# Four seven-product steps per panel, a six-slot ring in the feed-forward stage, and 36 low halves made by an accumulating transfer

## The chip, the cores and the metric

One Trainium2 chip, one core. The metric is device time in microseconds of one execution of the whole program, from inputs in HBM to the output in HBM. The kernel before takes 3272.08 us (median of 3 runs, 3271.72 to 3272.53). The matrix engine is called PE here, VectorE DVE, ScalarE ACT, GpSimd POOL; SP issues the loads.

## What is computed

Three transformer blocks over 256 tokens of width 2048, all in float32: two layers of the first kind, one of the second. Cut to what matters:

```python
def hybrid_layer(x, mem, ...):                 # twice
    u = rms_norm(x, norm_g) @ w_in             # 2048 -> 15944 columns
    ...                                        # four branches a, b, c, m on 512 columns each
    for n, (y, z) in enumerate(...):
        branch = y * silu(z)
        merged += sigmoid(gate_all[:, :, n]) * (branch @ w_branch[n])   # gates: 4 x 2048 columns of u
    return x + merged @ w_out

def hybrid_layer_2(x, ...):                    # once
    ...                                        # two attentions, gates, w_o
    gt, up = split(rms_norm(x, g_ffn) @ w_gate_up)    # 2 x 5632 columns
    return x + (silu(gt) * up) @ w_down
```

Every weight is used once, on 256 tokens. 610 MB come in from HBM.

## The kernel before

**The work is a stream of chunks.** `stream()` (L76) lists blocks of weight columns in the order of use. A plain block is 512 columns wide and is loaded in chunks of two 128-row tiles, 128x1024 elements, 512 KB. PE works in float32r. So that the product has float32's accuracy, each chunk is split: ACT rounds it to float32r into `w_hi` (L1148), and DVE writes the remainder, raw minus `w_hi`, into `w_lo` (L1452). Three matmuls then stand for one exact one: high by high, low by high, high by low (L1127, and `three`, L1044, in panels). A chunk of a plain block is 2 row tiles x 2 token tiles x 3 = 12 matmuls of 512 columns.

**Panels.** 19 blocks are panels, 1024 columns wide: five in each of the two layers (gates of branches c, m, b; `("panel", l, br, n)`) and nine in the feed-forward stage (`("panel", FF, "f", j)`, 512 columns of gate beside 512 of up). A panel has 16 row tiles, taken as eight steps of two. A step is a 2x2 by 2x2 product of tiles: 128 tokens twice, two row tiles, 512 columns twice. In the plain form it takes 8 products, 24 matmuls, as two units `row` of 12. In the seven-product form (Winograd's) it takes 7 products, 21 matmuls, as four units: `low` (6 matmuls), `first` (3), `sums13` (6) and `sums24` (6). Its price lies elsewhere: DVE makes four sums of weight tiles (`sums13` L1434, `sums24` L1439 and L1440), and these are split like other chunks. In elements per partition a plain step has 2048 to split, a seven-product step 3584, beside the 2048 of sums. Steps 1, 3 and 5 have this form before (`SEVEN`, L35). The token side needs sums too, "forms": POOL makes them (`x_forms`, L1852), ACT rounds them (L1392), DVE writes the remainder (`form_lo`, L1755), once for each layer and once for the feed-forward stage, and PE waits for all of them at the first unit of the first panel (L1071).

**The order of a stage.** In the layers a panel is followed by two merge blocks of two chunks each (`branch @ w_branch` for the 1024 columns whose gates the panel made), then the next panel: one "layer period". In the feed-forward stage down block j-2 (four blocks of two chunks: 8 chunks) comes before panel j: one "feed-forward period" is 8 down chunks and a panel. Before the first of these panels stand gate and up of j = 0 and 1 as plain blocks, then the down blocks of j = 0.

**Rings.** Raw chunks and split chunks lie in rings of four slots. From the first panel of a layer to its last merge the rings have six (`wide`, L136; `in_slots`, L185): the two further slots lie over memory that is idle then. A unit is split into the slot that the oldest unit leaves, so ACT and DVE may run 4 (or 6) units ahead of PE and no more. SP issues a load when the split that read its raw slot is done, and waits in order for that (L712 to L714).

**Work behind a unit.** `schedule()` (L223) lists by unit number what else is to be done. PE does it right behind that unit. ACT and DVE do it behind the split for which they had to wait for PE to finish that unit (`BEHIND`, L212), so four or six units later in their own order. This holds for the work at the end of a panel too: `stem` (ACT), `cross` (DVE L1457 to L1460), `gather` (DVE L1469), `silu_product` (L1475, L1479), the merges (L1541, L1543) and the adds of the down blocks (L1513). The forms of the feed-forward stage stand at `end_of("up", 0) + 4 + 6 * i` (L312).

**Counters.** `hi_done` and `lo_done` count the splits, `mm_done` the units that PE has finished. A wait for unit c's low half is `lo_done >= c + 1`.

Of the kernel before, what the change touches and what calls it, by code (L numbers as in the profile page):

```python
# [7 lines left out]
F32 = mybir.dt.float32  # L8
# [6 lines left out]
P = 128  # L15
# [4 lines left out]
H = 4  # L20
# [13 lines left out]
STEPS = KD // 2  # L34
SEVEN = (1, 3, 5)  # L35
N_FF = 5632 // NB
FF, FF_PLAIN = 3, 2
PANEL_EVENTS = (0, 1, FF)
HEADS2 = 8
NOPE, ROPE2 = 128, 64  # L40
# [15 lines left out]
class Block:  # L56


    def __init__(self, name, weights, col, pair, kk, kt, kind, width=NB):
        self.name, self.weights, self.col, self.pair = name, weights, col, pair  # L60
        self.kk, self.kt, self.kind, self.width = kk, kt, kind, width
        self.ck = 1 if width == WIDE else CK if width == NB else kt // 2
        self.first = 0
        self.wide = False
        self.g = self.before = None

    @property
    def chunks(self):
        return sum(4 if s in SEVEN else 2 for s in range(STEPS)) if self.kind == "panel" else self.kt // self.ck

# [5 lines left out]
def stream():  # L76
# [56 lines left out]
    for b in out:  # L133
        b.first = at
        at += b.chunks
        b.wide = (b.kind == "panel" and b.name[1] != FF) or (b.name[0] == "merge" and b.name[1] < DEPTH and ("panel", *b.name[1:3], b.name[3] // 2) in panels)  # L136
        b.before = tuple(uses)
        if b.kind == "panel":
            uses = [n + 1 for n in uses]
            g = 1  # L140
        else:
            g = b.g = 1 - g
            uses[g] += 1
# [7 lines left out]
def in_units():  # L151

    units, loads = [], []
    for b, blk in enumerate(BLOCKS):
        if blk.kind != "panel":
            for s in range(blk.chunks):
                units.append((b, "plain", s, len(loads)))
                loads.append((b, s))
            continue
        for s in range(STEPS):  # L160
            k0 = len(loads)
            loads += [(b, 2 * s), (b, 2 * s + 1)]
            if s in SEVEN:
                units += [(b, "low", s, k0 + 1), (b, "first", s, k0), (b, "sums13", s, None), (b, "sums24", s, None)]
            else:
                units += [(b, "row", 2 * s, k0), (b, "row", 2 * s + 1, k0 + 1)]
    return units, loads
# [11 lines left out]
LAST_PANEL = {l: max(b for b in PANELS if BLOCKS[b].name[1] == l) for l in PANEL_EVENTS}  # L179
FORMS_DONE = {l: len(SEVEN) * (i + 1) for i, l in enumerate(PANEL_EVENTS)}  # L180
FF_PANEL = {b: i for i, b in enumerate(b for b in PANELS if BLOCKS[b].name[1] == FF)}
STEM_ENDS = {SUMS_UNIT[b, SEVEN[-1]]: b for b in PANELS}

# [28 lines left out]
BEHIND = {c: range(max(R_BEHIND[c], 0), R_BEHIND[c + 1]) for c in range(N_CHUNKS)}  # L212
EXT_FIRST = {l: [min(c for c in range(FIRST_WIDE[l], N_CHUNKS) if U_SLOT[c] == k) for k in (4, 5)] for l in range(DEPTH)}
EXT_LOAD = {l: min(r for r, (b, _s) in enumerate(LOADS) if b >= FIRST_PANEL[l] and R_SLOT[r] >= RING) for l in range(DEPTH)}
BLOCK = {b.name: i for i, b in enumerate(BLOCKS)}
# [7 lines left out]
def schedule():  # L223
# [17 lines left out]
    for l in range(DEPTH):  # L241
# [28 lines left out]
        for h in range(H):  # L270
# [5 lines left out]
            at(c + 8, "tail", "b", l, h)  # L276
        for i in range(len(SEVEN)):
            at(r + 150 + 6 * i, "forms", l, i)
# [29 lines left out]
    for j in range(N_FF):  # L308
        for half in range(2):
            at((end_of("up", j) + 2 if j < FF_PLAIN else end_of("panel", FF, "f", j) + 4) + half, "h_feed", j, half)  # L310
    for i in range(len(SEVEN)):
        at(end_of("up", 0) + 4 + 6 * i, "forms", FF, i)  # L312
# [107 lines left out]
def hybrid_program(nc, x, mem_by_col, w_in, w_mem_kv, w_branch, w_out, w_in2, b_gate, w_uq, w_ukv, w_o_mla, w_o_dil, w_o2, w_gu, w_down,  # L420
                   pars_d, x_by_col, k_ident, k_levels, k_tables, k_dil, x_kept, mkv_kept, out):
    with ExitStack() as ctx:
# [129 lines left out]
        sums = over("sums", "arena", 0, [P, 2, 4, NB], F32)  # L552
        form_hi_in = over("form_hi_in", "arena", 8192, [P, len(SEVEN), 4, P], F32R)
        form_hi_ff = over("form_hi_ff", "arena", 4096, [P, len(SEVEN), 4, P], F32R)
        form_hi = {0: form_hi_in, 1: form_hi_in, FF: form_hi_ff}
        form_lo = over("form_lo", "tmp", 0, [P, len(SEVEN), 4, P], F32R)
        form = [tmp[:, 3072 + 512 * i:3584 + 512 * i].rearrange("p (f t) -> p f t", t=P) for i in range(2)]
# [30 lines left out]
        crossed, x_banks_free, wide_sig, hidden_ready = sem("crossed"), sem("x_banks_free"), sem("wide_sig"), sem("hidden_ready")  # L588
        hi_done, lo_done, mm_done = sem("hi_done"), sem("lo_done"), sem("mm_done")
        gm_free = [sem(f"gm_free{i}") for i in range(2)]  # L590
        pt_full, pt_hi = sem("pt_full"), sem("pt_hi")
# [115 lines left out]
        def _(sp):  # L707
            def load(r):
                b, s = LOADS[r]
                blk = BLOCKS[b]  # L710
                if R_PREV[r] >= 0:
                    sp.wait_ge(lo_done, SPLIT_OF[R_PREV[r]] + 1)  # L712
                    if LOADS[R_PREV[r]] in LOAD_SUMS:
                        sp.wait_ge(sums_done, 2 * LOAD_SUMS[LOADS[R_PREV[r]]] + 2)  # L714
                for l, first in EXT_LOAD.items():
                    if r == first:
                        sp.wait_ge(y_ready, Y_OF[("s_pv", "l", 2, HEADS2 - 1) if l == FF else ("s_pv", "m", l, H - 1)] + 1)
                k = R_SLOT[r]
                if b in FF_PANEL:
                    pair = weights[blk.weights].rearrange("(c p) (h n) -> c p h n", p=P, h=2)  # L720
                    to = slot_of(raw, raw_more, k).rearrange("p (h n) -> p h n", h=2)
                    sp.dma_start(to, pair[s, :, :, blk.col:blk.col + NB]).then_inc(raw_landed[k], 16)
                    return
                to = slot_of(raw, raw_more, k)[:, 0:blk.ck * blk.width].rearrange("p (j n) -> p j n", n=blk.width)
                sp.dma_start(to, cut(weights[blk.weights], blk.ck)[s, :, :, blk.col:blk.col + blk.width]).then_inc(raw_landed[k], 16)
# [17 lines left out]
            def back(l):  # L743
                sp.wait_ge(lo_done, SUMS_UNIT[LAST_PANEL[l], SEVEN[-1]] + 1)
                if l:
                    sp.wait_ge(x_saved, 64 * l)
                sp.dma_start(xs, rows(x[0] if l == 0 else x_kept)).then_inc(x_back, 16)
# [7 lines left out]
            def bring_mkv():  # L755
                sp.wait_ge(mkv_out, 16)
                sp.wait_ge(lo_done, end_of("merge", 0, "b", 3))
                sp.dma_start(arena[:, 11408:13456].rearrange("p (i n) -> p i n", n=NB),
                             mkv_kept.rearrange("i (t p) n -> p (i t) n", p=P)).then_inc(mkv_in, 16)
# [58 lines left out]
        def _(pe):  # L818
# [234 lines left out]
            def by_form(l, s, f):  # L1053
                i = SEVEN.index(s)
                return form_hi[l][:, i, f, :], form_lo[:, i, f, :]

            def panel(b, blk):
# [14 lines left out]
                for c in range(blk.first, blk.end):  # L1072
                    _b, what, s, _r = UNITS[c]
                    first, last = s == SEVEN[0], s == SEVEN[-1]
                    pe.wait_ge(lo_done, c + 1)
                    if what == "low":
# [22 lines left out]
            for b, blk in enumerate(BLOCKS):  # L1099
# [6 lines left out]
                for s in range(blk.chunks):  # L1106
# [6 lines left out]
                    if blk.name == ("a_qi", 0):  # L1113
                        pe.wait_ge(first_fed, s + 1)
                        pe.wait_ge(ident_in, 16)
                    pe.wait_ge(lo_done, c + 1)
                    for j in range(blk.ck):
# [15 lines left out]
        def _(act):  # L1133
            A = nc.scalar.activation

            def split(c):
# [5 lines left out]
                if U_PREV[c] >= 0:  # L1142
                    act.wait_ge(mm_done, U_PREV[c] + 1)
                for l in range(DEPTH):
                    if c in EXT_FIRST[l]:
                        act.wait_ge(y_ready, Y_OF["norm", "b", l, H - 1] + 1)
                        act.wait_ge(o_squared, NORM_OF["norm", "b", l, H - 1] + 1)
                A(high_of(c)[:, 0:size_of(c)], source_of(c), ACT.Copy).then_inc(hi_done, 1)  # L1148

            def stem(b):  # L1150
                _, l, br, m = BLOCKS[b].name
                act.wait_ge(mm_done, SUMS_UNIT[b, SEVEN[-1]] + 1)
                if b == FIRST_PANEL[l]:
# [264 lines left out]
        def _(dve):  # L1418
# [9 lines left out]
            def sums13(n, r):  # L1428
                for k in (r, r + 1):
                    dve.wait_ge(raw_landed[R_SLOT[k]], 16 * (R_COUNT[k] + 1))  # L1430
                if n >= 2:
                    dve.wait_ge(lo_done, SUMS_UNIT[SUMS[n - 2]] + 1)
                q = pair_of(r)
# [8 lines left out]
            def split(c):  # L1442
                b, what, s, r = UNITS[c]
                if what == "low":
                    sums13(SUMS_N[b, s], r - 1)
# [344 lines left out]
        def _(pool):  # L1790
# [61 lines left out]
            def x_forms(l, i):  # L1852

                k, n = 2 * SEVEN[i], FORM_N["forms", l, i]
                if n >= 2:
# [25 lines left out]
            for l in range(DEPTH):  # L1881
# [25 lines left out]
                for i in range(H):  # L1907
                    if i < len(SEVEN):
                        x_forms(l, i)
                    output_norm()  # L1910
# [36 lines left out]
            pool.wait_ge(y_ready, Y_OF["s_pv", "l", 2, HEADS2 - 1] + 1)  # L1947
            for i in range(len(SEVEN)):
                x_forms(FF, i)


# [34 lines left out]
```

## Time and profile before

| | |
|---|---|
| median of 3 runs | 3272.08 us |
| the profiled execution | 3272.8 us |
| its span, first to last instruction | 3271.0 us |
| PE busy | 3258.1 us |
| DVE, ACT, POOL busy | 2203.4, 1638.9, 321.3 us |
| moved by DMA | 619.77 MB, 189 GB/s |

A matmul's row shows 0.39 us, but they are pipelined: the next starts 0.23 us later. So a group's count times its mean duration is more than the time it takes, and times of PE are read from starts. The same holds less strongly for DVE and ACT: a row of 1.22 us is followed by the next start after 1.13 us.

### The profile page before, as it was taken

To read this page: it belongs to the slowest core of one execution; us is meant where nothing else is said; L and a number is where in the kernel's file an instruction comes from. 1 tells how busy PE (TensorE), PEld (TensorE's weight loads), DVE (VectorE), ACT (ScalarE), POOL (GpSimd) and SP (SyncE) were. 2 spreads that over 40 slices of the span, in tenths; PEclk is the share of its full clock that TensorE was granted. 3 is DMA by queue.
4 is the path that set the end of the run, shared out by engine and by line. 5 is a ranking of instruction groups with operands and counts; after the bars stand their busy time and mean duration, and the time that the engine had idled before them with its cause. 6 is when DMAs were issued, how large, how long until landed. Compare 5 with 4: busy or idle time off the path is not lost.

```text
span 3271.0 us, 39924 instructions
## 1 busy us (share of the span) xinstructions
PE 3258.1 (100%) x15091; PEld 2699.7 (83%) x15091; DVE 2203.4 (67%) x2476; ACT 1638.9 (50%) x2085; POOL 321.3 (10%) x282
## 2 busy tenths in 40 slices
PE   8999999999999999999999999999999999999999
PEld 7888888888888888888888888888888888888887
DVE  5466655588865656555888655575555578888887
ACT  6444445455544444454555445455444455555554
POOL 0111241100000102411000011160000100000000
PEclk9999999999999999999999999999999999999999
DMA  8665565666666655556665675554565656556655
GB/s 300 191 185 166 165 177 162 188 206 193 217 193 205 182 167 166 173 164 186 202 211 183 208 226 170 172 179 144 193 192 183 186 187 204 187 194 204 194 193 180
DMA packets 303808, 619.77 MB, mean 189 GB/s; under 512 B 24961, under 2 KB 29441, under 8 KB 302465
## 3 DMA queue, kind: packets, MB, share of 16 engines
q1 hardware_dynamic: 303616, 617.22, 60.9%
q8 instruction: 120, 1.97, 0.2%
q14 instruction: 72, 0.58, 0.1%
HBM read 609.80 MB, written 7.34 MB: 189 GB/s over the span
## 4 chain that ended last, share of the span: by engine, by line
PE 100%; DMA 0%; DVE 0%; ACT 0%; SPq 0%; issue 0%
PE G L1127 69%; PE X L1048 6%; PE X L1046 6%; PE X L1047 6%; PE X L826 2%; PE G L1048 2%; PE G L1047 2%; PE G L1046 2%; PE X L942 1%; PE X L914 1%; PE G L1121 1%; PE X L969 0%; PE X L968 0%; PE X L935 0%; PE X L916 0%; PE X L889 0%
## 5 line engine op out<-in xcount | busy, mean ns | idle before, releaser
L1452 DVE TENSOR_TENSOR w_lo<-raw,w_hi 128x1024 fp32r<-128x1024 f32 (+1 forms) x1016 | 1236.9, 1223 | 942.2 <-ACT w_hi L1148 915.4
L1148 ACT ACTIVATE w_hi<-raw 128x1024 fp32r<-128x1024 f32 (+1 forms) x1016 | 1052.8, 1041 | 1265.3 <-PE G L1127 1129.0
L1127 PE MATMUL G<-w_hi,xh 128*128 128x512 f32 x1984 | 796.0, 401 | 0.0
L1127 PE MATMUL G<-w_hi,xl 128*128 128x512 f32 x1984 | 775.0, 391 | 0.0
L1127 PE MATMUL G<-w_lo,xh 128*128 128x512 f32 x1984 | 772.7, 389 | 0.0
L1127 PE MATMUL G<-w_hi,yh 128*128 128x512 f32 x1256 | 499.3, 398 | 8.5 <-DVE w_lo L1452 8.5
L1127 PE MATMUL G<-w_hi,yl 128*128 128x512 f32 x1256 | 491.2, 391 | 0.0
L1127 PE MATMUL G<-w_lo,yh 128*128 128x512 f32 x1256 | 490.0, 390 | 0.0
L1127 PEld LDWEIGHTS G<-w_hi,xl 128*128 128x128 f32 x1984 | 372.3, 188 | 81.0
L1127 PEld LDWEIGHTS G<-w_hi,xh 128*128 128x128 f32 x1984 | 372.9, 188 | 73.9 <-issue 2.7
L1127 PEld LDWEIGHTS G<-w_lo,xh 128*128 128x128 f32 x1984 | 373.3, 188 | 72.2
L1048 PE MATMUL X<-w_hi,xl 128*128 128x512 f32 x754 | 293.8, 390 | 0.0
L1046 PE MATMUL X<-w_hi,xh 128*128 128x512 f32 x754 | 293.8, 390 | 0.0
L1047 PE MATMUL X<-w_lo,xh 128*128 128x512 f32 x754 | 293.6, 389 | 0.0
L1127 PEld LDWEIGHTS G<-w_hi,yh 128*128 128x128 f32 x1256 | 236.6, 188 | 55.0 <-issue 8.4
L1127 PEld LDWEIGHTS G<-w_hi,yl 128*128 128x128 f32 x1256 | 236.3, 188 | 50.7
L1127 PEld LDWEIGHTS G<-w_lo,yh 128*128 128x128 f32 x1256 | 236.7, 188 | 47.0
L1047 PEld LDWEIGHTS X<-w_lo,xh 128*128 128x128 f32 x754 | 141.5, 188 | 30.3
L1048 PEld LDWEIGHTS X<-w_hi,xl 128*128 128x128 f32 x754 | 141.5, 188 | 30.0
L1046 PEld LDWEIGHTS X<-w_hi,xh 128*128 128x128 f32 x754 | 141.5, 188 | 29.8
L1148 ACT ACTIVATE w_hi<-sums 128x1024 fp32r<-128x1024 f32 x90 | 95.6, 1062 | 135.9 <-PE X L1048 97.8
L1452 DVE TENSOR_TENSOR w_lo<-sums,w_hi 128x1024 fp32r<-128x1024 f32 x90 | 108.5, 1222 | 38.7 <-ACT w_hi L1148 38.7
(261 smaller groups left out, 3164.3 us busy)
## 6 DMA issues: line engine op xcount, KB each, us to landing
raw<-in_w_in SPq DMA_DIRECT2D x572, 512.0 KB, 3.6
raw<-in_w_gate_up SPq DMA_DIRECT2D x176, 512.0 KB, 4.1
raw<-in_w_down SPq DMA_DIRECT2D x88, 512.0 KB, 4.5
raw<-in_w_out SPq DMA_DIRECT2D x64, 512.0 KB, 4.2
raw_more<-in_w_in SPq DMA_DIRECT2D x52, 512.0 KB, 4.4
raw<-in_w_branch SPq DMA_DIRECT2D x48, 512.0 KB, 3.8
raw<-in_w_mem_kv SPq DMA_DIRECT2D x32, 512.0 KB, 6.3
raw<-in_w_o SPq DMA_DIRECT2D x32, 512.0 KB, 3.6
```

Of the source, the lines that this page charges most:

```text
L826: mm = M.transpose(PT[i % 2][0:n, col:col + P], src, ident[:])
L914: mm = M.matmul(PS[:, t * T:(t + 1) * T], qk_t[:, t * P:(t + 1) * P], qk_t[:, T:2 * T], start=True, stop=br != "l")
L942: mm = M.matmul(PO[:, t * P:(t + 1) * P], p_t[:, a, t * P:(t + 1) * P], v(a), start=(a == 0), stop=(a == TT - 1))
L1046: M.matmul(bank, of_h, high_of(c)[:, cols], start=start, stop=False)
L1047: M.matmul(bank, of_h, low_of(c)[:, cols], start=False, stop=False)
L1048: return M.matmul(bank, of_l, high_of(c)[:, cols], start=False, stop=stop)
L1121: mm = M.matmul(G[blk.g][0:blk.width, 0, 0:T], ringed(w, blk, c)[:, j, :], a[:, blk.kk + k, :], start=(k == 0 and q == 0), stop=(k == blk. ...
L1127: mm = M.matmul(G[blk.g][:, t, :], a[:, blk.kk + k, tok], ringed(w, blk, c)[:, j, :], start=(k == 0 and q == 0), stop=(k == blk.kt - 1 and ...
L1148: A(high_of(c)[:, 0:size_of(c)], source_of(c), ACT.Copy).then_inc(hi_done, 1)
L1452: V.tensor_tensor(low_of(c)[:, 0:n], source_of(c), high_of(c)[:, 0:n].bitcast(F32), ALU.subtract).then_inc(lo_done, 1)
```

## The change

- Panels have their seven-product form in steps 1, 2, 4 and 5 instead of 1, 3 and 5 (`SEVENS`); the last panel of each layer has it in 1, 2 and 4 (`LIGHT`). Buffers and work for a fourth form are added, in each layer and in the feed-forward stage.
- The rings have six slots in the feed-forward stage too, from its first panel on (`b.wide`); slots 4 and 5 of the split ring are first used four units after the start of that panel.
- Of the down blocks of j = 0 to 8 each second chunk, 36 in all, is split in another way: ACT writes `w_hi`, and then the raw chunk once more, rounded and negated, into the low slot (`scale=-1.0`); POOL then issues a transfer that adds the raw chunk onto it. DVE leaves these chunks out. PE, and the load that reuses the raw slot, wait for the transfer (`lo_added`). `lows()` corrects all waits on `lo_done` for the chunks left out.

The diff, cut; replacements of `SEVEN` by its new names and of counts by `lows()` that change nothing else are left out:

```diff
@@ -35 +34,0 @@
-SEVEN = (1, 3, 5)
@@ -38,0 +38,3 @@
+SEVENS = {0: (1, 2, 4, 5), 1: (1, 2, 4, 5), FF: (1, 2, 4, 5)}
+LIGHT = {("panel", l, "b", 1): (1, 2, 4) for l in range(DEPTH)}
+FORMS = max(len(s) for s in SEVENS.values())
@@ -61,0 +64 @@
+        self.seven = LIGHT.get(name, SEVENS[name[1]]) if kind == "panel" else ()
@@ -69 +72 @@
-        return sum(4 if s in SEVEN else 2 for s in range(STEPS)) if self.kind == "panel" else self.kt // self.ck
+        return sum(4 if s in self.seven else 2 for s in range(STEPS)) if self.kind == "panel" else self.kt // self.ck
@@ -136 +139 @@
-        b.wide = (b.kind == "panel" and b.name[1] != FF) or (b.name[0] == "merge" and b.name[1] < DEPTH and ("panel", *b.name[1:3], b.name[3] // 2) in panels)
+        b.wide = b.kind == "panel" or (b.name[0] == "down" and b.name[1] > 0) or (b.name[0] == "merge" and b.name[1] < DEPTH and ("panel", *b.name[1:3], b.name[3] // 2) in panels)
@@ -163 +166 @@
-            if s in SEVEN:
+            if s in blk.seven:
@@ -180 +183 @@
-FORMS_DONE = {l: len(SEVEN) * (i + 1) for i, l in enumerate(PANEL_EVENTS)}
+FORMS_DONE = {l: sum(len(SEVENS[m]) for m in PANEL_EVENTS[:i + 1]) for i, l in enumerate(PANEL_EVENTS)}
@@ -182 +185,2 @@
-STEM_ENDS = {SUMS_UNIT[b, SEVEN[-1]]: b for b in PANELS}
+STEM_END = {b: SUMS_UNIT[b, BLOCKS[b].seven[-1]] for b in PANELS}
+STEM_ENDS = {c: b for b, c in STEM_END.items()}
@@ -213,2 +217,11 @@
-EXT_FIRST = {l: [min(c for c in range(FIRST_WIDE[l], N_CHUNKS) if U_SLOT[c] == k) for k in (4, 5)] for l in range(DEPTH)}
-EXT_LOAD = {l: min(r for r, (b, _s) in enumerate(LOADS) if b >= FIRST_PANEL[l] and R_SLOT[r] >= RING) for l in range(DEPTH)}
+ADDED = [c for c, (b, _w, s, _r) in enumerate(UNITS) if BLOCKS[b].name[0] == "down" and BLOCKS[b].name[1] < N_FF - 2 and s == 1]
+ADDED_N = {c: sum(U_SLOT[d] == U_SLOT[c] for d in ADDED if d < c) for c in ADDED}
+
+
+def lows(n):
+
+    return n - sum(1 for c in ADDED if c < n)
+
+
+EXT_FIRST = {l: [min(c for c in range(FIRST_WIDE[l], N_CHUNKS) if U_SLOT[c] == k) for k in (4, 5)] for l in PANEL_EVENTS}
+EXT_LOAD = {l: min(r for r, (b, _s) in enumerate(LOADS) if b >= FIRST_PANEL[l] and R_SLOT[r] >= RING) for l in PANEL_EVENTS}
...
@@ -553,2 +566,2 @@
-        form_hi_in = over("form_hi_in", "arena", 8192, [P, len(SEVEN), 4, P], F32R)
-        form_hi_ff = over("form_hi_ff", "arena", 4096, [P, len(SEVEN), 4, P], F32R)
+        form_hi_in = over("form_hi_in", "arena", 8192, [P, FORMS, 4, P], F32R)
+        form_hi_ff = over("form_hi_ff", "arena", 4096, [P, FORMS, 4, P], F32R)
@@ -556 +569 @@
-        form_lo = over("form_lo", "tmp", 0, [P, len(SEVEN), 4, P], F32R)
+        form_lo = over("form_lo", "tmp", 0, [P, FORMS, 4, P], F32R)
@@ -589,0 +603 @@
+        lo_negative, lo_added = sem("lo_negative"), [sem(f"lo_added{i}") for i in range(WIDE_RING)]
@@ -712 +726,4 @@
-                    sp.wait_ge(lo_done, SPLIT_OF[R_PREV[r]] + 1)
+                    if SPLIT_OF[R_PREV[r]] in ADDED_N:
+                        sp.wait_ge(lo_added[U_SLOT[SPLIT_OF[R_PREV[r]]]], 16 * (ADDED_N[SPLIT_OF[R_PREV[r]]] + 1))
+                    else:
+                        sp.wait_ge(lo_done, lows(SPLIT_OF[R_PREV[r]] + 1))
...
@@ -1116 +1133,4 @@
-                    pe.wait_ge(lo_done, c + 1)
+                    if c in ADDED_N:
+                        pe.wait_ge(lo_added[U_SLOT[c]], 16 * (ADDED_N[c] + 1))
+                    else:
+                        pe.wait_ge(lo_done, lows(c + 1))
@@ -1144 +1164 @@
-                for l in range(DEPTH):
+                for l in PANEL_EVENTS:
@@ -1146,2 +1166,6 @@
-                        act.wait_ge(y_ready, Y_OF["norm", "b", l, H - 1] + 1)
-                        act.wait_ge(o_squared, NORM_OF["norm", "b", l, H - 1] + 1)
+                        if l == FF:
+                            act.wait_ge(y_ready, Y_OF["s_pv", "l", 2, HEADS2 - 1] + 1)
+                            act.wait_ge(x_sq_done, 16)
+                        else:
+                            act.wait_ge(y_ready, Y_OF["norm", "b", l, H - 1] + 1)
+                            act.wait_ge(o_squared, NORM_OF["norm", "b", l, H - 1] + 1)
@@ -1148,0 +1173,2 @@
+                if c in ADDED_N:
+                    A(low_of(c)[:, 0:size_of(c)], source_of(c), ACT.Copy, scale=-1.0).then_inc(lo_negative, 1)
@@ -1152 +1178 @@
-                act.wait_ge(mm_done, SUMS_UNIT[b, SEVEN[-1]] + 1)
+                act.wait_ge(mm_done, STEM_END[b] + 1)
...
@@ -1443,0 +1470,2 @@
+                if c in ADDED_N:
+                    return
...
@@ -1908 +1936 @@
-                    if i < len(SEVEN):
+                    if i < len(SEVENS[l]):
...
@@ -1949,0 +1978,3 @@
+            for i, c in enumerate(ADDED):
+                pool.wait_ge(lo_negative, i + 1)
+                V.dma_start(low_of(c).bitcast(F32), source_of(c), accum_op=ALU.add).then_inc(lo_added[U_SLOT[c]], 16)
```

## Rows read from the trace of the kernel before

**Rows 1.** The page: busy time of each engine, transfers, chain that ended last

```profile
PE 3258.1 (100%) x15091; PEld 2699.7 (83%) x15091; DVE 2203.4 (67%) x2476; ACT 1638.9 (50%) x2085; POOL 321.3 (10%) x282
...
PE 100%; DMA 0%; DVE 0%; ACT 0%; SPq 0%; issue 0%
```

**Rows 2.** Waits of PE, whole span: waited for, us in total, times, longest

```profile
PE G L1127 <- DVE w_lo L1452: 8.5, 1, 8.5
```

**Rows 3.** Timeline of PE, first feed-forward panel: start us, us, instruction

```profile
2672.06 0.40 PE L1047 MATMUL G<-w_lo,xh 128*128 128x512 f32 x1
2682.32 0.40 PE L1047 MATMUL G<-w_lo,xh 128*128 128x512 f32 x1
...
2706.70 0.39 PE L1127 MATMUL G<-w_hi,yh 128*128 128x512 f32 x1
2706.93 0.39 PE L1127 MATMUL G<-w_lo,yh 128*128 128x512 f32 x1
```

**Rows 4.** Chain that ended last: plain blocks behind two panels, start us, us

```profile
693.03 11.00 PE G L1127 x48
2706.86 13.61 PE G L1127 x60
```

**Rows 5.** Windows of one layer period and one feed-forward period

```profile
745.84:798.81 52.97, 52.97 (x232) 43.36 (x232) 45.43 (x46) 29.91 (x32) 0.00 (x0) 1.00 0.63 200
2771.28:2835.66 64.38, 64.38 (x288) 53.15 (x288) 54.07 (x56) 34.16 (x38) 0.00 (x0) 1.00 0.61 197
```

**Rows 6.** Timeline of DVE, a seven-product step in layer 0

```profile
774.96 1.22 DVE L1434 TENSOR_TENSOR sums<-raw 128x1024 f32<-128x1024 f32 x1
776.09 1.22 DVE L1452 TENSOR_TENSOR w_lo<-raw,w_hi 128x1024 fp32r<-128x1024 f32 x1
777.23 0.69 DVE L1439 TENSOR_TENSOR sums<-raw,sums 128x512 f32<-128x512 f32 x1
777.95 0.69 DVE L1440 TENSOR_TENSOR sums<-raw,sums 128x512 f32<-128x512 f32 x1
778.56 0.69 DVE L1452 TENSOR_TENSOR w_lo<-raw,w_hi 128x512 fp32r<-128x512 f32 x1
779.16 2.35 DVE L1452 TENSOR_TENSOR w_lo<-sums,w_hi 128x1024 fp32r<-128x1024 f32 x2
781.43 1.22 DVE L1452 TENSOR_TENSOR lo_more<-raw,hi_more 128x1024 fp32r<-128x1024 f32 x1
```

**Rows 7.** Timeline of DVE, first panel of layer 0, behind its first seven-product step

```profile
655.16 1.22 DVE L1541 TENSOR_TENSOR gates<-G,gates 128x1024 f32<-128x1024 f32 x1
656.42 1.23 DVE L1543 TENSOR_TENSOR arena<-gates,arena 128x1024 f32<-128x1024 f32 x1
657.56 2.36 DVE L1452 TENSOR_TENSOR w_lo<-raw,w_hi 128x1024 fp32r<-128x1024 f32 x2
```

**Rows 8.** Timeline of DVE, behind gather and merges of the next panel

```profile
708.88 1.22 DVE L1452 TENSOR_TENSOR w_lo<-raw_more,w_hi 128x1024 fp32r<-128x1024 f32 x1
```

**Rows 9.** Timeline of ACT around the first down blocks

```profile
2642.56 1.06 ACT L1148 ACTIVATE w_hi<-raw 128x1024 fp32r<-128x1024 f32 x1 [1.66 <-PE G L1127]
2645.28 1.06 ACT L1148 ACTIVATE w_hi<-raw 128x1024 fp32r<-128x1024 f32 x1 [1.66 <-PE G L1127]
...
2672.09 2.01 ACT L1148 ACTIVATE w_hi<-raw 128x1024 fp32r<-128x1024 f32 x2 [0.31 <-PE X L1048]
```

**Rows 10.** DMA issues: xcount, KB each, median us from issue to landing

```profile
raw<-in_w_gate_up SPq DMA_DIRECT2D x128, 512.0 KB, 4.2
raw<-in_w_down SPq DMA_DIRECT2D x64, 512.0 KB, 4.7
...
x_kept<-arena SPq DMA_DIRECT2D x8, 512.0 KB, 5.4
out<-arena SPq DMA_DIRECT2D x4, 512.0 KB, 2.8
mkv_kept<-arena SPq DMA_DIRECT2D x1, 1024.0 KB, 7.9
```

**Rows 11.** Timeline of DVE at the start of the first feed-forward panel

```profile
2647.52 0.68 DVE L1755 TENSOR_TENSOR form_lo<-tmp,form_hi_ff 128x512 fp32r<-128x512 f32 x1
...
2664.34 1.22 DVE L1452 TENSOR_TENSOR w_lo<-raw,w_hi 128x1024 fp32r<-128x1024 f32 x1
2665.48 0.68 DVE L1439 TENSOR_TENSOR sums<-raw,sums 128x512 f32<-128x512 f32 x1
```

**Rows 12.** Timeline of POOL, last norms of branch b in layer 0

```profile
592.69 0.71 POOL L1801 TENSOR_SCALAR stat<-stat 128x2 f32<-128x2 f32 x1 [9.63 <-ACT core L1335]
...
608.43 0.71 POOL L1801 TENSOR_SCALAR stat<-stat 128x2 f32<-128x2 f32 x1 [14.24 <-ACT core L1335]
```

More of the change, by code:

```diff
@@ L276, in schedule @@
             at(c + 8, "tail", "b", l, h)
-        for i in range(len(SEVEN)):
+        for i in range(len(SEVENS[l])):
             at(r + 150 + 6 * i, "forms", l, i)
@@ L310, in schedule @@
             at((end_of("up", j) + 2 if j < FF_PLAIN else end_of("panel", FF, "f", j) + 4) + half, "h_feed", j, half)
-    for i in range(len(SEVEN)):
+    for i in range(len(SEVENS[FF])):
         at(end_of("up", 0) + 4 + 6 * i, "forms", FF, i)
@@ L743, in back @@
             def back(l):
-                sp.wait_ge(lo_done, SUMS_UNIT[LAST_PANEL[l], SEVEN[-1]] + 1)
+                sp.wait_ge(lo_done, lows(STEM_END[LAST_PANEL[l]] + 1))
                 if l:
@@ L756, in bring_mkv @@
                 sp.wait_ge(mkv_out, 16)
-                sp.wait_ge(lo_done, end_of("merge", 0, "b", 3))
+                sp.wait_ge(lo_done, lows(end_of("merge", 0, "b", 3)))
                 sp.dma_start(arena[:, 11408:13456].rearrange("p (i n) -> p i n", n=NB),
@@ L1053, in by_form @@
             def by_form(l, s, f):
-                i = SEVEN.index(s)
+                i = SEVENS[l].index(s)
                 return form_hi[l][:, i, f, :], form_lo[:, i, f, :]
@@ L1073, in panel @@
                     _b, what, s, _r = UNITS[c]
-                    first, last = s == SEVEN[0], s == SEVEN[-1]
-                    pe.wait_ge(lo_done, c + 1)
+                    first, last = s == blk.seven[0], s == blk.seven[-1]
+                    pe.wait_ge(lo_done, lows(c + 1))
                     if what == "low":
@@ L1115, in _ @@
                         pe.wait_ge(ident_in, 16)
-                    pe.wait_ge(lo_done, c + 1)
+                    if c in ADDED_N:
+                        pe.wait_ge(lo_added[U_SLOT[c]], 16 * (ADDED_N[c] + 1))
+                    else:
+                        pe.wait_ge(lo_done, lows(c + 1))
                     for j in range(blk.ck):
@@ L1431, in sums13 @@
                 if n >= 2:
-                    dve.wait_ge(lo_done, SUMS_UNIT[SUMS[n - 2]] + 1)
+                    dve.wait_ge(lo_done, lows(SUMS_UNIT[SUMS[n - 2]] + 1))
                 q = pair_of(r)
@@ L1852, in x_forms @@
             def x_forms(l, i):
-                k, n = 2 * SEVEN[i], FORM_N["forms", l, i]
+                k, n = 2 * SEVENS[l][i], FORM_N["forms", l, i]
                 if n >= 2:
@@ L1947, in _ @@
             pool.wait_ge(y_ready, Y_OF["s_pv", "l", 2, HEADS2 - 1] + 1)
-            for i in range(len(SEVEN)):
+            for i in range(len(SEVENS[FF])):
                 x_forms(FF, i)
+            for i, c in enumerate(ADDED):
+                pool.wait_ge(lo_negative, i + 1)
+                V.dma_start(low_of(c).bitcast(F32), source_of(c), accum_op=ALU.add).then_inc(lo_added[U_SLOT[c]], 16)
 def packed(inputs):
```

## The prediction

> **What bounds the kernel now.** The page first: PE is busy for 3258.1 of 3271.0 us, and the chain that ended last is PE for 100% of its length [rows 1]. The waits of PE come next: in the whole span it waited once, 8.5 us, at the start [rows 2]. So only PE's own instructions make the time, and the change is worth what it takes from them, less every wait that it brings. The other engines matter as far as they come near PE. In a layer period DVE is busy for 45.43 of 52.97 us, in a feed-forward period for 54.07 of 64.38, ACT for 29.91 and 34.16 [rows 5]. 0.2% of the time, 6.5 us, is about what a measurement can tell from no change.
>
> **PE: the steps.** Starts of matmuls lie 0.227 us apart, and a chunk of 12 takes 2.72 [rows 3] (48 in 11.00 us say 0.229 [rows 4]). The same matmul of two neighbouring seven-product steps recurs after 10.26 us, with one plain step between them [rows 3]. The plain step is 24 x 0.227 = 5.44, which leaves 4.82 for the other; one step in the new form saves 0.62 us. 17 of the 19 panels get one more (the last panel of each layer keeps three): 17 x 0.62 = **10.5 us** less. By the bare count, 3 x 0.227 = 0.68 each, it would be 11.6; I take 10.5, because it is read from the steps themselves.
>
> **DVE in the layers.** A seven-product step costs DVE 781.43 - 774.96 = 6.47 us, a plain one two splits at 1.135, 2.27 [rows 6]: 4.20 more, for 4.82 instead of 5.44 us of PE. A layer period then wants some 45.4 + 4.2 = 49.6 of 52.3 us, so in sum DVE still keeps up. But steps 1 and 2 are now neighbours, just where gather and merges lie. Behind them DVE is free at 708.88 [rows 8], with PE at the merge chunks since 693.03 [rows 4]. PE reaches step 2 at 693.03 + 10.9 + 5.44 + 4.82 = 714.2, and its last two units at 716.2 and 717.6. DVE makes step 2 from 708.88 to 715.35, its units at 711.2, 713.1, 714.2 and 715.35: 2.0 us early at the narrowest. The first panel of a layer is tighter. It starts at 693.03 - 5 x 5.44 - 3 x 4.82 = 651.4; step 2 begins at 661.65 and wants `sums13` at 663.7 and `sums24` at 665.1. DVE is free at 657.56 [rows 7] and has them at 662.9 and 664.0, 0.8 and 1.1 early; steps 4 and 5 leave about 0.6. No wait in my forecast, but the margin is thin.
>
> **Forms.** A fourth one costs POOL some 4.5 us, ACT 0.6, DVE 0.7, three times. In the layers POOL does it between two norms; it idled 14.24 us there [rows 12], so it is hidden, as are ACT's and DVE's shares. In the feed-forward stage it is not. The fourth stands at `end_of("up", 0) + 22`, two units before the panel, and PE waits for it at the panel's first unit. In the trace the third ended at 2648.2, long before. The fourth would come behind the split of the panel's third unit, where L1439 stands now at 2665.48 [rows 11], and end at 2666.2; the panel starts at 2706.86 - 41.7 = 2665.1 [rows 4]. **1.1 us** more.
>
> **ACT and DVE in the feed-forward stage.** A period gives DVE one step more (4.20) and four splits less (4 x 1.135 = 4.54), ACT 1.5 rounds at 1.0 for the step and four for the negated chunks: ACT 34.2 + 5.5 = 39.7, DVE 53.7, both of 63.8 us. Six slots instead of four let them run two units further ahead. So no wait from either.
>
> **The accumulating transfer.** The trace of before has none. Its length L, from ACT's end to its semaphore, decides the rest. It reads 512 KB and the 512 KB it adds to, and writes 512 KB, beside loads that keep the engines 61% busy [rows 5]. From below: 2.8 us, a store of 512 KB with nothing beside it [rows 10]. Nearest rows: 5.4 for such a store beside loads, 7.9 for a store of 1024 KB [rows 10]. From above: no row ends it; two of the 5.4 in turn, 10.8, is my upper end. I take 6.5, between the two nearest, nearer to the first since the bytes that leave are 512 KB.
> With six slots ACT starts a chunk 0.25 us after PE has left its slot, and two rounds take 2.0 [rows 9]; PE needs the chunk five units later, 13.6. So L may be 11.3, and the four transfers of a period, 5.4 us apart, need not even overlap. The load that waits for the raw slot lands 4.7 later [rows 10] and is still some 10 us early. No cost there.
> The down blocks of j = 0 still have four slots. There PE needs the chunk after three units, 8.16, and L may be 5.9. Chunk 5 of that stage waits longer: its load waits for the transfer of chunk 1, so it is ready after 2.3 + L + 4.7 + 2.0 + L, and PE is there after 7 units and two turns of the hidden state, 20.2. The loss is 2L - 11.2, which covers the first wait too: **1.8 us** for L = 6.5, 0 from 5.6 down, 10.4 for 10.8.
>
> The Trainium skill (DMA: Bandwidth & Descriptors, section "Anatomy of one DMA") gives 2.0 us plus bytes over 436 GB/s for a plain transfer that POOL issues, 3.2 us here as an estimate; by it the sum would lose nothing in these blocks and be rival A. No row of this case shows such a transfer.
>
> **Sum.** -10.5 + 1.1 + 1.8 = -7.6 us. The profiled execution took 3272.8, 0.7 over the median, and its parts are read from it; from the median of 3272.1 I get **3264.5 us**.
>
> **Rivals.**
> *A: the transfer is short*, L up to 5.6. For it: it goes from SBUF to SBUF, and the store with nothing beside it took 2.8. Against it: loads are beside it, and a load took 4.7. 3272.1 - 10.5 + 1.1 = 3262.7; with the bare count of matmuls 3261.6.
> *B: the transfer takes twice a load*, L = 9.4, since it reads two streams. The loss is 7.6: 3270.3. If the load behind it doubles too, chunk 5 waits 12.3 and the time is 3275.0.
> *C, slower: the transfer holds PE in every period.* The place is the second chunk of each of the 32 later down blocks; from L = 11.3 on PE waits once in a period for the first of them. It decides before that: the j = 0 blocks alone eat the gain at 2L - 11.2 = 9.4, L = 10.3. With L = 14 they cost 16.8, the eight periods 8 x 2.7 = 21.6: 3301. For it: nothing here bounds how fast the engines add. Against it: 1024 KB moved in 7.9.
> *D: DVE is late in the layers*, behind steps 1 and 2. For it: margins of 0.6 to 2.0 us. Against it: the starts above. The eight panels would give back what they save, 5.0: 3269.5.
> *E: the seven-product form saves nothing on PE*; then 3272 to 3275. Its 4.82 against 5.44 speaks against it.
>
> **Chances.** My forecast 0.48, A 0.22, B 0.10, C 0.09, D 0.08, E 0.03. Faster by over 0.2% means under 3265.5: A, and the forecast with L up to 7.0 (0.38): 0.60. Same: the rest of the forecast, B, D and E, 0.31. Slower by over 0.2% (over 3278.6): C, 0.09. The range reaches from A by the bare count, less the spread of the runs, to B with both doubled: 3261 to 3275; it leaves out C and the ends.
>
> **What would show it.** PE should have 51 matmuls less. Its waits should show a row for L1127, some 2 us at the down blocks of j = 0 (right if two waits at most, none in later periods), and one of about 1 us at the start of the first feed-forward panel for `form_lo`. A layer period should read 52.3 us, a feed-forward period 63.8. The new queue's issues should show 36 transfers, 6.5 us to landing; that number settles A, B and C. DVE should be busy for some 49.6 us of a layer period, and PE should have no wait for `w_lo` or `lo_more` in panels. I am wrong if the periods keep their length, if PE waits in layer panels, or if 36 waits for transfers appear.

## The result, and the profile after

The changed kernel takes 3276.9 us, 4.7 more than the kernel before (3272.2, 20 runs each): ratio 1.0015, 95% interval 1.0009 to 1.0021. The forecast was 3264.5, in a range of 3261 to 3275. The change's profiled execution took 3276.3, with a span of 3274.5, 3.5 over the span of before. The engines' line of its page, against [rows 1]:

```profile
PE 3253.7 (99%) x15040; PEld 2690.5 (82%) x15040; DVE 2231.4 (68%) x2528; ACT 1696.0 (52%) x2158; POOL 365.0 (11%) x333
```

The waits of PE over its whole span (who waits for what on which engine: us, times, longest), against [rows 2]:

```profile
PE G L1147 <- DVE w_lo L1480: 8.3, 1, 8.3
PE G L1147 <- DMA w_lo<-raw: 6.1, 2, 4.3
PE X L1063 <- DVE yl L1581: 1.2, 3, 0.7
PE X L843 <- DVE yl L1581: 0.9, 2, 0.5
```

PE has its 51 matmuls less, and busy time fell by only 4.4 us where they are worth 10.5: so the matmuls that are left cost more. Beside that stand 8.2 us of new waits (`yl` is the low half of the tokens' side). (Lines have moved: L1147 was L1127, L1063 to L1065 were L1046 to L1048, L1480 was L1452, L1172 was L1148.)

The chain of the changed kernel, in order of time (start us, us, what; cut), tells where the stages stand; against [rows 4]:

```profile
691.98 10.93 PE G L1147 x48
744.16 11.00 PE G L1147 x48
...
848.70 10.93 PE G L1147 x48
930.47 13.65 PE G L1147 x60
...
2605.48 32.69 PE G L1147 x144
2710.35 13.70 PE G L1147 x60
2774.90 13.72 PE G L1147 x60
...
3225.30 13.73 PE G L1147 x60
3242.66 27.45 PE G L1147 x120
```

The same points stand at 2609.79, 2706.86 and 3222.06 us before. So the changed kernel is 4.3 us ahead where the plain blocks of the feed-forward stage begin. It is 3.5 behind at the end of the first feed-forward panel: 7.8 lost in one stretch. Over the eight periods that follow it gains 0.25, where 5 were due. The whole loss lies in the feed-forward stage.

### The profile page after: what moved, and what is told of

It is laid out like the page before. It is cut to its first block, busy times and chain, and to the rows that moved or that the text cites. A ratio compares the mean times of both kernels' runs of the same rounds, so it can differ in the third digit from the quotient of the medians.

```text
span 3274.5 us, 40087 instructions
## 1 busy us (share of the span) xinstructions
PE 3253.7 (99%) x15040; PEld 2690.5 (82%) x15040; DVE 2231.4 (68%) x2528; ACT 1696.0 (52%) x2158; POOL 365.0 (11%) x333
## 4 chain that ended last, share of the span: by engine, by line
PE 97%; DMA 1%; issue 0%; DVE 0%; ACT 0%; SPq 0%; ACTq 0%; DVEq 0%
PE G L1147 67%; PE X L1063 6%; PE X L1065 6%; PE X L1064 6%; PE X L843 2%; PE G L1065 2%; PE G L1064 2%; PE G L1063 2%; PE X L959 1%; PE X L931 1%; PE G L1141 1%; DMA w_lo<-raw 0%; PE X L986 0%; PE X L985 0%; PE X L952 0%
## 5 line engine op out<-in xcount | busy, mean ns | idle before, releaser
L1480 DVE TENSOR_TENSOR w_lo<-raw,w_hi 128x1024 fp32r<-128x1024 f32 x869 | 1058.1, 1222 | 882.1 <-ACT w_hi L1172 859.2
L1172 ACT ACTIVATE w_hi<-raw 128x1024 fp32r<-128x1024 f32 x890 | 917.9, 1035 | 1149.0 <-PE G L1147 1014.3
L1147 PE MATMUL G<-w_hi,xh 128*128 128x512 f32 x1984 | 796.0, 401 | 0.0
L1147 PE MATMUL G<-w_hi,xl 128*128 128x512 f32 x1984 | 775.0, 391 | 0.0
L1147 PE MATMUL G<-w_lo,xh 128*128 128x512 f32 x1984 | 772.7, 389 | 0.0
L1147 PE MATMUL G<-w_hi,yh 128*128 128x512 f32 x1152 | 458.8, 398 | 14.3 <-DVE w_lo L1480 8.3
L1147 PE MATMUL G<-w_hi,yl 128*128 128x512 f32 x1152 | 451.3, 392 | 0.0
L1147 PE MATMUL G<-w_lo,yh 128*128 128x512 f32 x1152 | 449.9, 391 | 0.0
L1147 PEld LDWEIGHTS G<-w_hi,xl 128*128 128x128 f32 x1984 | 372.3, 188 | 80.9
L1147 PEld LDWEIGHTS G<-w_hi,xh 128*128 128x128 f32 x1984 | 372.9, 188 | 73.9 <-issue 2.7
L1147 PEld LDWEIGHTS G<-w_lo,xh 128*128 128x128 f32 x1984 | 373.4, 188 | 72.3
L1147 PEld LDWEIGHTS G<-w_hi,yh 128*128 128x128 f32 x1152 | 217.4, 189 | 57.8 <-issue 8.2
L1147 PEld LDWEIGHTS G<-w_hi,yl 128*128 128x128 f32 x1152 | 217.0, 188 | 47.1
L1147 PEld LDWEIGHTS G<-w_lo,yh 128*128 128x128 f32 x1152 | 217.6, 189 | 43.4
L1063 PE MATMUL X<-w_hi,xh 128*128 128x512 f32 x500 | 195.6, 391 | 0.9 <-DVE yl L1581 0.9
L1065 PE MATMUL X<-w_hi,xl 128*128 128x512 f32 x500 | 195.3, 391 | 0.0
L1064 PE MATMUL X<-w_lo,xh 128*128 128x512 f32 x500 | 194.9, 390 | 0.0
L1172 ACT ACTIVATE w_hi<-sums 128x1024 fp32r<-128x1024 f32 x104 | 109.3, 1060 | 108.6 <-DVE sums L1466 36.2
L1480 DVE TENSOR_TENSOR w_lo<-raw_more,w_hi 128x1024 fp32r<-128x1024 f32 x91 | 107.7, 1199 | 50.9 <-ACT w_hi L1172 50.6
L1172 ACT ACTIVATE hi_more<-raw 128x1024 fp32r<-128x1024 f32 x98 | 93.1, 970 | 73.7 <-PE X L1065 54.3
L1172 ACT ACTIVATE w_hi<-raw_more 128x1024 fp32r<-128x1024 f32 x96 | 99.2, 1043 | 54.2 <-PE X L1065 26.2
```

Of the source, the lines that this page charges most:

```text
L1063: M.matmul(bank, of_h, high_of(c)[:, cols], start=start, stop=False)
L1064: M.matmul(bank, of_h, low_of(c)[:, cols], start=False, stop=False)
L1065: return M.matmul(bank, of_l, high_of(c)[:, cols], start=False, stop=stop)
L1147: mm = M.matmul(G[blk.g][:, t, :], a[:, blk.kk + k, tok], ringed(w, blk, c)[:, j, :], start=(k == 0 and q == 0), stop=(k == blk.kt - 1 and ...
L1480: V.tensor_tensor(low_of(c)[:, 0:n], source_of(c), high_of(c)[:, 0:n].bitcast(F32), ALU.subtract).then_inc(lo_done, 1)
```

## The experiments

**Four parts taken by themselves.** e1 empties the list of chunks that get a transfer, so that DVE makes all low halves:

```diff
-ADDED = [c for c, (b, _w, s, _r) in enumerate(UNITS) if BLOCKS[b].name[0] == "down" and BLOCKS[b].name[1] < N_FF - 2 and s == 1]
+ADDED = []
```

> The changed kernel with no accumulating transfer: DVE makes all low halves. My theory: the change gains 3.8 us in the layers and loses it in the feed-forward stage: 6.1 us of waits for transfers and 1.9 us of low clock behind them at the down blocks of j = 0, 1.2 us of waits in later periods, and 0.4 us in each period because matmuls from slots 4 and 5 start later. Then this kernel is at 3276.9 - 6.1 - 1.9 - 1.2 + 1.1 (the fourth form, no longer covered) = 3268.8, with matmuls in the feed-forward periods still 0.2288 us apart. Rival 1: DVE needs the transfers; with 58.2 of 64.2 us it comes late in each period, PE shows waits for w_lo in the feed-forward panels, and the time is 3277 or more. Rival 2: it is the transfers that slow the matmuls; then their distance falls to 0.227 and the time is about 3265.

Measured: 3267.8 us, ratio 0.9986 (0.9977 to 0.9995). The 36 transfers alone cost 9.1 us (3276.9 against 3267.8), and without them the change makes the kernel 4.4 us faster than before. A feed-forward period of e1, with the columns of [rows 5]:

```profile
2767.93:2832.11 64.18, 64.18 (x285) 52.52 (x285) 57.88 (x61) 35.85 (x40) 0.00 (x0) 1.00 0.62 197
```

DVE is busy for 57.88 us of it, near the 58.2 of the sum, and PE has no wait in any period. So rival 1 of that text is out: with six slots DVE did not need relief. The eight periods take 64.1 to 64.2 us and not 63.8; rival 2 is out too, since the longer distance of the matmuls stayed.

e2 is the kernel before with the change's line for `b.wide` and nothing else (`SEVENS` all `(1, 3, 5)`, `LIGHT` and `ADDED` empty).

> The kernel before with six slots in the feed-forward stage and nothing else (steps 1, 3 and 5, no transfer). My theory: matmuls whose operand is another memory than that of the unit before cost more, so each of the eight feed-forward periods is 0.4 us longer, the first panel 0.4 and the end 0.3: 3272.2 + 4 = 3276. Rival: the ring costs nothing, the longer distance of matmuls comes from the transfers or from the form of the steps: 3272.2.

Measured: 3275.9, ratio 1.0011 (1.0002 to 1.0020). Six slots cost 3.7 us by themselves, without a wait. One of the periods, 64.4 us long before:

```profile
2771.81:2836.55 64.74, 64.74 (x288) 53.16 (x288) 54.01 (x56) 34.25 (x38) 0.00 (x0) 1.00 0.63 195
```

e3 leaves the four transfers of j = 0 out (`0 < BLOCKS[b].name[1] < N_FF - 2`).

> The changed kernel with the transfers only from j = 1 on, where the ring has six slots; DVE makes the four of j = 0. My theory: the waits of 6.1 us and the low clock of 1.9 us go, the fourth form's 1.1 us appears: 3276.9 - 8.0 + 1.1 = 3270.0, with waits of some 1 us left for yl in later periods. Rival: the loss is in every period (load on the DMA engines, rounds on ACT), and the time stays at 3275 or more.

Measured: 3270.8, ratio 0.9995 (0.9987 to 1.0004). Four of the 36 transfers cost 6.1 us of the 9.1; the other 32 cost 3.0, more than I had put down. The 6.1 is net: with these four gone, PE waits 1.2 us for the fourth form, which their waits had covered.

e4 has the change in the layers only.

> Only the panels of the two layers as in the change; the feed-forward stage as before (steps 1, 3, 5, four slots, no transfer). My theory: the layers gain 8 steps of 0.62 and lose 0.6 at each end of a layer, where gather now stands six units behind: 5.05 - 1.24 = 3.8 less than before, 3268.4. Rival: the gain of the layers is taken back later by other waits: 3272.

Measured: 3268.6, ratio 0.9989 (0.9980 to 0.9998). The layers alone gain 3.6 us, where 3.8 were expected.

**Were the six slots needed?** e5 is e1 with four slots in the feed-forward stage (the old line for `b.wide`).

> The seven-product steps of the change everywhere, but four slots in the feed-forward stage and no transfer. My theory: the six slots there cost 3.7 us and give nothing back, since DVE with 58.2 of 63.8 us keeps up; then 3267.8 - 3.7 = 3264.1 (also 3272.2 - 10.5 + 1.2 + 1.2). Rival: with steps 1 and 2 as neighbours DVE needs the lead of six slots; PE shows waits for w_lo in each feed-forward panel, and the time is 3270 or more.

Measured: 3287.4, ratio 1.0046 (1.0033 to 1.0058). My theory fell here. Among the waits of PE over the whole span of e5 this row is new:

```profile
PE G L1063 <- DVE w_lo L1480: 8.0, 36, 0.3
```

One of its periods, with the columns of [rows 5]:

```profile
2705.53:2771.70 66.17, 65.26 (x286) 52.13 (x285) 58.18 (x61) 35.48 (x40) 0.00 (x0) 1.00 0.58 188
```

PE waits in each of the nine panels four times, and a period takes 66.2 us. DVE's sum of 58.2 fits in 63.8, but with four slots the lead is too short to carry it over the two neighbouring steps: the chain of this period leaves PE twice, for DVE's `sums` and the splits behind them. A sum over a period says nothing of a stretch of ten microseconds within it. The row of waits names 0.9 of the 2.4 us that the period loses against 63.8; most of the rest is that the matmuls around such a wait start 0.3 us or more apart instead of 0.23. e5 makes the ring of raw chunks smaller too, and in other periods the chain also runs through a load (3.88 us at 3005.66); which of the two rings matters is not separated. The six slots cost 3.7 us by themselves, yet without them this order of steps is 19.6 us slower (3287.4 against 3267.8 in e1).

**Why do six slots make matmuls slower?** The tail of the changed kernel shows it. From 3244 to 3256 us its DMA share is 0.00, so no transfer of any kind is beside it, and from 3256.1 us on there is no split. Timeline of PE, first matmul of each unit of 12 (start us, us, instruction):

```profile
3245.26 0.39 PE L1147 MATMUL G<-hi_more,yh 128*128 128x512 f32 x1
...
3248.00 0.40 PE L1147 MATMUL G<-w_hi,yh 128*128 128x512 f32 x1
...
3250.77 0.39 PE L1147 MATMUL G<-w_hi,yh 128*128 128x512 f32 x1
...
3253.49 0.39 PE L1147 MATMUL G<-w_hi,yh 128*128 128x512 f32 x1
...
3256.21 0.39 PE L1147 MATMUL G<-w_hi,yh 128*128 128x512 f32 x1
...
3258.93 0.40 PE L1147 MATMUL G<-hi_more,yh 128*128 128x512 f32 x1
...
3261.70 0.39 PE L1147 MATMUL G<-hi_more,yh 128*128 128x512 f32 x1
...
3264.44 0.40 PE L1147 MATMUL G<-w_hi,yh 128*128 128x512 f32 x1
```

Units that follow one of the same memory within the first four slots take 2.72 us, as all did before. The first behind a change of memory takes 2.77 (3248.00, 3258.93), the second in the further slots 2.74 (3261.70). That is 0.12 per round of six in plain blocks. A feed-forward period of e2 has 30 units, five rounds, and is 0.36 us longer than before, so in panels, whose units have 3 to 12 matmuls, a round costs less. e8 gives e2 four slots again, but 0, 1, 4 and 5. Its main line (the rest passes it the units from the first feed-forward panel on):

```diff
-        k = min(range(0, ring, width), key=lambda x: last[x]) if i % width == 0 else slots[-1] + 1
+        k = min((0, 1, 4, 5) if i in four else range(0, ring, width), key=lambda x: last[x]) if i % width == 0 else slots[-1] + 1
```

> The ring-only kernel with four slots in the feed-forward stage again, but slots 0, 1, 4 and 5, so that units alternate between the two memories in pairs while ACT and DVE lead by four. My theory: it is the change of the memory that costs, about 0.05 us at the first unit behind each change and 0.02 at the next unit in the further slots; four slots in two memories then cost one and a half times what six did: 3272.2 + 5.5 = 3277.7. Rival: the number of slots, or how far ACT and DVE work ahead, costs; then 3272.2.

Measured: 3277.7, ratio 1.0016 (1.0007 to 1.0025). The lead is four again and the cost is 5.2 us against 3.7, nearly half as large again as with six slots. The intervals of the two ratios overlap, but the traces agree with the medians: the eight periods average 64.40 us before, 64.76 in e2 and 64.93 in e8, with 92 changes of memory from the first feed-forward panel on in e2 and 137 in e8. So the cost goes with the change of memory, not with the number of slots or the work ahead of PE. Why PE takes longer there stays open.

**The waits at the ends.** e6 is e1 with the feed-forward forms five units apart (`4 + 5 * i`).

> The changed kernel without transfers, with the forms of the feed-forward stage five units apart instead of six, so that the fourth is three units earlier. My theory: PE's wait of 1.2 us for form_lo goes, 3267.8 - 1.2 = 3266.6. Rival: another wait at the start of that panel takes its place, 3267.8.

Measured: 3266.4, ratio 0.9981 (0.9972 to 0.9990). PE's 1.2 us for `form_lo`, which e1 shows, are gone.

e7 is e1 with merges 2 and 3 of branch b kept out of `b.wide`.

> The changed kernel without transfers, with the last two merges of each layer in four slots, so that gather, the merges and the turns of merged stand four units behind as before and not six. My theory: PE's waits for yl behind the last panel of a layer go (0.9 us in the trace) and the 0.6 us longer stretch at each end of a layer with them: 3267.8 - 1.2 = 3266.6. Rival: the longer stretch has to do with the steps of the last panel (1, 2, 4), not with the slots: 3267.8.

Measured: 3268.0, ratio 0.9987 (0.9978 to 0.9995), with the same two waits for yl. The edit does more than was meant: in DVE's program `blk.wide` also picks the gates that a merge multiplies by (L1557), so these merges read the wrong gates, leave out the wait for the right ones, and the output of e7 is wrong. It speaks for the place of gather alone. By the program gather stood four units behind the panel's last unit there, six in e1, and in both behind a split that waits for that last unit; in e7 it began at 904.69, right behind the split of 903.55. So the number of units by which gather stands back was not the cause. DVE of the changed kernel at the end of layer 0:

```profile
902.74 1.23 DVE L1480 TENSOR_TENSOR w_lo<-raw,w_hi 128x1024 fp32r<-128x1024 f32 x1 [1.50 <-ACT w_hi L1172]
903.88 2.35 DVE L1497 TENSOR_TENSOR gates<-X,gates 128x1024 f32<-128x1024 f32 x2
```

PE had ended the panel at 901.4, but gather (L1497) stands behind a split that could start only then. Before, the panel ended at 904.3 and gather began at once:

```profile
904.51 2.36 DVE L1469 TENSOR_TENSOR gates<-X,gates 128x1024 f32<-128x1024 f32 x2 [0.48 <-PE X L1048]
```

There the slots fell so that it stood behind a split that waits for a unit two before the panel's last. e9 is e6 with that one gather per layer moved (cut; its old place is left out in these two layers):

```diff
+                if c in early:
+                    read_out(early[c])
                 split(c)
```

> The kernel with earlier forms and no transfers, and in DVE's program the gather of the last panel of each layer ahead of the split behind which it stands. With the last merges in four slots the longer stretch stayed, so my theory of the distance fell. Theory now: gather stands behind a split that itself waits for the end of that panel, 2.3 us later, where in the kernel before the slots fell so that three units' work stood behind an earlier split; moved ahead, PE's waits for yl go and each end of a layer is 0.6 us shorter: 3266.4 - 1.2 = 3265.2. Rival: ACT's rounds, not DVE's gather, hold the turns of merged; then 3266.4.

Measured: **3264.9**, ratio 0.9977 (0.9968 to 0.9985), the fastest of all, 7.7 us under the kernel before: all the steps of the change and none of its transfers. In layer 0 gather now begins when PE releases it, and the waits of PE are the one at the start and no other:

```profile
902.62 2.36 DVE L1497 TENSOR_TENSOR gates<-X,gates 128x1024 f32<-128x1024 f32 x2 [0.34 <-PE X L1065]
...
PE G L1147 <- DVE w_lo L1480: 8.7, 1, 8.7
```

**What do the later transfers cost, and how?** The chain of e3 before one of its four waits for yl (2.0 us in all):

```profile
2900.29 8.88 DMA lo_more<-raw
...
2909.18 3.12 DMA raw<-in_w_gate_up
...
2915.49 1.22 DVE lo_more L1480
2916.71 0.60 DVE yl L1581
...
2920.38 0.61 DVE yl L1581
...
2921.23 0.47 PE X L1063
```

The raw slot is held until the transfer has ended; the load behind it feeds the first seven-product step; DVE must split that before it gets to the low half of the hidden state, which stands behind that split; and PE waits for that half at the panel's first unit. Its first matmul then takes 0.47 us instead of 0.23, so such a wait costs more than its own length. e10 is e3 with transfers in the first two down blocks only (`BLOCKS[b].name[2] < 2`), whose raw slots are refilled earlier.

> Transfers only from j = 1 on and only in the first two of the four down blocks of each j: 16 instead of 32. My theory: the 3.0 us that the 32 cost come through the raw slots of the last two blocks, whose next loads feed the first seven-product step and, behind it on DVE, the low half of the hidden state for which PE waits at the start of the panel; without these two PE shows no wait for yl in the feed-forward stage and the time is that of the kernel with none, 3267.8, or up to 0.5 more. Rival: each transfer costs alike, by its traffic or ACT's second round; then 3267.8 + 1.5 = 3269.3.

Measured: 3267.8, ratio 0.9985 (0.9976 to 0.9994). 16 transfers cost nothing, neither by their traffic nor by ACT's second round. The 3.0 us come with the other 16, in the last two blocks, and with them goes every wait for yl in the feed-forward stage. These 16 were not run alone.

## Why the prediction was wrong, point by point

The forecast was 12.4 us too low. What failed is the sum's list of costs: the transfer was sized at 1.8 us and cost 6.1 in waits, and four costs were put at nothing that together came to some 8 us: six slots, the clock behind a wait, the turns of the hidden state, and the end of a layer.

**Right: the step's worth.** e4 measures it alone. Its chain has these two rows, with four panels and their merges between the first and the second:

```profile
618.52 32.67 PE G L1147 x144
...
849.17 10.93 PE G L1147 x48
```

That is 230.65 us, against 233.17 before (618.50 to 851.67), 0.63 for each panel. **Right: DVE in the layers.** A period of the changed kernel shows DVE busy for 49.37 of 52.29 us, without a wait of PE; rival D is out:

```profile
744.16:796.45 52.29, 52.29 (x229) 42.81 (x229) 49.37 (x51) 31.13 (x34) 0.00 (x0) 1.00 0.61 202
```

**Right, but not to be seen: the fourth form.** e1 has it with 1.2 us (1.1 was said). In the changed kernel DVE wrote the remainder at 2663.48, while PE stood waiting for a transfer.

**Mis-sized: the transfer.** The term was 2L - 11.2 with L = 6.5 and a load of 4.7. The chain at the down blocks of j = 0:

```profile
2638.26 1.06 ACT w_hi L1172
2639.32 0.95 ACT w_lo L1174
2640.27 0.30 issue
2640.57 7.91 DMA w_lo<-raw
...
2648.50 5.48 DMA raw<-in_w_down
...
2654.97 1.05 ACT w_lo L1174
2656.03 0.37 issue
2656.39 8.01 DMA w_lo<-raw
...
2664.45 4.61 PE G L1147 x12
```

From ACT's end to the landing L is 8.2 and then 8.4, and the load between took 5.5. The same working gives 2.3 + 8.2 + 5.5 + 2.0 + 8.4 - 20.2 = 6.2; the waits are 6.1. The chain of dependences was the right one, its links were longer. By the Trainium skill's fit (DMA: Bandwidth & Descriptors, "Anatomy of one DMA"), an estimate of 3.2 us for a plain transfer of this size, rival A would have won. The measurement of the accumulating one decides: over twice as long.

**Left out: the clock behind the wait.** The last row above is 12 matmuls in 4.61 us instead of 2.72. The windows around it (the columns of [rows 5]; the clock is third from the right):

```profile
2660.00:2664.00 4.00, 0.17 (x1) 0.00 (x0) 4.00 (x5) 1.58 (x2) 0.00 (x0) 1.00 0.68 141
2664.00:2668.00 4.00, 3.55 (x9) 2.82 (x10) 1.46 (x3) 0.00 (x0) 0.00 (x0) 0.61 0.53 160
2668.00:2676.00 8.00, 8.00 (x36) 6.54 (x35) 5.92 (x6) 4.23 (x6) 0.00 (x0) 0.98 0.73 249
```

PE stood still for 4.3 us, and the granted clock of the next stretch is 0.61: most of it at 1.2 GHz. That is 1.9 us on top of the wait by the chain, 1.7 by the starts of the matmuls (2664.45 to 2668.90), of which 0.1 goes with any restart: behind the wait of 1.8 us, at a clock of 1.00, 12 matmuls took 2.86. The trace of before had one wait only, but it showed this cost, and I did not read it. Behind its 8.5 us at the start the first 12 matmuls took 5.20 us, 0.43 apart as behind the wait above, though the clock's column shows 1.00 there:

```profile
8.46 0.77 PE L1127 MATMUL G<-w_hi,yh 128*128 128x512 f32 x1 [8.46 <-DVE w_lo L1452]
...
12.87 0.63 PE L1127 MATMUL G<-w_lo,yh 128*128 128x512 f32 x1
13.30 0.53 PE L1127 MATMUL G<-w_hi,yl 128*128 128x512 f32 x1
13.66 0.39 PE L1127 MATMUL G<-w_hi,yh 128*128 128x512 f32 x1
```

The Trainium skill (TensorE: Matmul & The Clock Gate, "Part 1") has the clock at one of two levels by how busy the engine was; these rows agree, with matmuls 0.43 us apart behind the long wait and 0.23 otherwise.

**Costed at nothing: the six slots.** "Six slots instead of four let them run two units further ahead. So no wait from either" was true of waits, and I asked nothing else of them. They cost 0.36 us in each period, 3.7 in all (e2). This could be read before: the layers had six slots already, and 48 matmuls took 11.00 us there, 60 took 13.61 in the feed-forward stage [rows 4]. I had noted 0.229 beside 0.227 and not asked why.

**Left out: the turns of the hidden state in six slots.** "Lands 4.7 later and is still some 10 us early" looked at the step that the load feeds. It did not look at what DVE does behind that split, the low half of the turned (transposed) hidden state: 1.2 us of waits in this trace, 3.0 us of time in e3's runs against e1's.

**Left out: the end of a layer,** 0.6 us twice, where the phase of the slots decides behind which split gather stands.

In sum, against the span of before and rounded as the traces show them: -10.5 for the steps, 6.1 + 1.9 for the transfers of j = 0, 1.2 for the later ones, 3.7 for six slots, 1.2 for the ends of the layers: 3.6, where the spans differ by 3.5. That the two agree to 0.1 is luck. By the length of the eight periods (514.95 us in the changed kernel, 512.97 in e1) the later transfers cost 2.0 and not 1.2, the clock's term may be 1.6, and the medians differ by 4.7. Rival B's transfer of 9.4 us comes nearest in mechanism, with a loss of 7.6 there; what it missed is the slots, the clock and the two small waits. Rival C, the transfer holding PE in every period, did not happen. The range ended at 3275 because each of its cases changed one term, while four terms that I had at nothing all went the same way.

## What to carry to other kernels

Before work is moved from one engine to a transfer, check that the engine was late at all: here DVE was near full, but only a stretch of it was critical, and the lead of six slots alone covered that. A transfer in a ring holds the slot it reads as well as the one it writes, so follow the load that refills the slot, and everything that stands behind its consumer. When a ring is enlarged, look at matmul starts and at where "behind unit e" now falls, not only at waits; where PE is the bound, 0.6% more on each of its periods (64.76 us against 64.40) outweighs most waits.

## What was not expected of the hardware

- An accumulating transfer of 512 KB within SBUF took a median of 7.0 us into `w_lo` from `raw` and 5.2 from `raw_more`, beside loads of 4.2 to 5.5; into `lo_more` it was 8.1 and 5.4. The two sources differ in memory and in the moment of issue; which one matters stays open.

```profile
w_lo<-raw POOLq DMA_DIRECT2D x21, 512.0 KB, 7.0
...
lo_more<-raw POOLq DMA_DIRECT2D x7, 512.0 KB, 8.1
...
w_lo<-raw_more POOLq DMA_DIRECT2D x5, 512.0 KB, 5.2
```

- Where the weights of a plain block lie in another SBUF tensor than those of the unit before, the 12 matmuls of the unit take 0.05 us more, and those of the unit after it in the further slots 0.02 more, with nothing waiting.
- A wait of 4.3 us cost PE another 1.6 to 1.9 through its clock; one of 1.8 us, at the first transfer of the same blocks, left the granted clock at 1.00.
